# Two mixers: the recurrent branch moved ahead of the last softmax, and two output blocks placed between the attention heads

## The reference

```
z = h @ w_in[l]
xr, yr, q, k, v = jnp.split(z, splits, axis=-1)
lru = rg_lru(causal_conv(xr, conv_w[l], conv_b[l]), gate_a_w[l], ...) * jax.nn.gelu(yr)
att = diff_attention(q, k, v, positions, ...)
x = x + g1 * (jnp.concatenate([lru, att], axis=-1) @ w_out[l])

# rg_lru: r, i sigmoid gates of the convolved x
log_a = -RG_C * r * jax.nn.softplus(-lam)
a = jnp.exp(log_a)
mult = jnp.sqrt(-jnp.expm1(2.0 * log_a))
_, h = lax.associative_scan(_lin_rec, (a, mult * (i * x)), axis=1)

# attention, per head: two softmaxes over masked scores
p = jax.nn.softmax(jnp.where(mask, s, neg), axis=-1)
pd = p[:, :, 0] - lam * p[:, :, 1]
o = rmsnorm(pd @ v, subln_g) * (1.0 - lambda_init)
```

## Time and profile before

| | us |
|---|---|
| median of 3 runs | 2181.72 |
| lowest and highest run | 2180.49, 2182.75 |
| the profiled execution | 2178.4 |
| its span, first instruction to last | 2176.5 |
| TensorE busy in the span | 2032.2 (93%) |
| VectorE busy | 1736.3 (80%) |
| ScalarE busy | 1250.9 (57%) |
| GpSimd busy | 50.0 (2%) |

### The profile page before, as it was taken

One profiled execution on the slowest core, in us unless ns is written; L12 is line 12 of the kernel. 1 busy time (PEld: TensorE's weight loads), 2 busy tenths in 40 slices (PEclk: granted clock), 3 DMA queues, 4 the chain that ended last, 5 costly groups with the idle time before them and its releaser, 6 DMA issues. The chain is left out here.

```text
span 2176.5 us, 31581 instructions
## 1 busy us (share of the span) xinstructions
PE 2032.2 (93%) x12420; PEld 1775.3 (82%) x12421; DVE 1736.3 (80%) x1989; ACT 1250.9 (57%) x1258; POOL 50.0 (2%) x87
## 2 busy tenths in 40 slices
PE   6999998978799989899999879999999999999996
PEld 6889996967699979699988768888888888788885
DVE  6758886786588877678787658898989898889886
ACT  5654444632354455643445647777777777777774
POOL 0000001000000000000000000000000000000000
PEclk9999999997699999999999979999999999999998
DMA  6347861201377634287864229998989898999894
GB/s 247 135 185 283 304 225 64 95 21 40 136 278 264 251 122 173 97 298 292 306 236 141 97 86 352 337 367 337 365 336 366 331 374 331 352 341 374 340 367 171
DMA packets 79069, 534.08 MB, mean 245 GB/s; under 512 B 11648, under 2 KB 13056, under 8 KB 15216
## 3 DMA queue, kind: packets, MB, share of 16 engines
q1 hardware_dynamic: 71440, 481.04, 58.9%
q0 software_dynamic: 7376, 51.25, 6.4%
q10 hardware_dynamic: 144, 0.26, 0.0%
HBM read 531.47 MB, written 1.05 MB: 245 GB/s over the span
## 5 line engine op out<-in xcount | busy, mean ns | idle before, releaser
L2586 DVE TENSOR_TENSOR weights_lo<-ring,weights_hi 128x2048 fp32r<-128x2048 f32 x288 | 656.6, 2291 | 94.7 <-ACT weights_hi L2580 93.0
L2580 ACT CAST weights_hi<-ring 128x2048 fp32r<-128x2048 f32 x288 | 550.8, 1916 | 153.4 <-PE bank L2730 71.6
L658 PE MATMUL bank<-acts_hi,weights_hi 128*128 128x256 f32 x1600 | 460.3, 288 | 17.2 <-DVE acts_lo L395 11.7
L373 DVE TENSOR_TENSOR weights_lo<-ring,weights_hi 128x2048 fp32r<-128x2048 f32 x162 | 370.4, 2290 | 119.0 <-ACT weights_hi L365 117.4
L658 PE MATMUL bank<-acts_lo,weights_hi 128*128 128x256 f32 x1600 | 454.2, 284 | 0.0
L658 PE MATMUL bank<-acts_hi,weights_lo 128*128 128x256 f32 x1600 | 454.1, 284 | 0.0
L365 ACT CAST weights_hi<-ring 128x2048 fp32r<-128x2048 f32 x162 | 308.8, 1909 | 251.0 <-PE bank L658 223.2
L658 PEld LDWEIGHTS bank<-acts_hi,weights_hi 128*128 128x128 f32 x1600 | 305.5, 191 | 24.4 <-issue 18.3
L2730 PE MATMUL bank<-weights_hi,xg_hi 128*128 128x512 f32 x768 | 307.5, 400 | 5.4 <-DVE xg_lo L2850 3.9
L658 PEld LDWEIGHTS bank<-acts_lo,weights_hi 128*128 128x128 f32 x1600 | 305.4, 191 | 2.6 <-issue 1.4
L658 PEld LDWEIGHTS bank<-acts_hi,weights_lo 128*128 128x128 f32 x1600 | 305.2, 191 | 0.0
(11 more groups left out here) (441 smaller groups left out, 2666.4 us busy)
## 6 DMA issues: line engine op xcount, KB each, us to landing
ring<-in_experts SPq DMA_DIRECT2D x288, 1024.0 KB, 5.1
ring<-in_dense SPq DMA_DIRECT2D x162, 1024.0 KB, 4.9
ada<-in_ada POOLq DMA_DIRECT2D x48, 1024.0 KB, 5.1
silu_c<-in_c SPq DMA_DIRECT2D x3, 512.0 KB, 6.3
resid<-in_x SPq DMA_DIRECT2D x1, 1024.0 KB, 6.6
out<-resid SPq DMA_DIRECT2D x2, 512.0 KB, 2.6
cst<-in_consts SPq DMA_DIRECT2D x1, 649.5 KB, 9.1
kh<-in_rwkv_g SPq DMA_DIRECT2D x1, 512.0 KB, 7.2
```

What stands on the lines that cost most here:

```text
L373: nc.vector.tensor_tensor(split[1][:, n % SPLITS, :], ring[:, n % RING, :], split[0][:, n % SPLITS, :].bitcast(F32), ALU.subtract).then_in ...
L658: ins = nc.tensor.matmul(bank[:, f * T:(f + 1) * T], split[w][:, m % SPLITS, k * 256 + f * P:k * 256 + (f + 1) * P], acts[x][:, k, :], sta ...
L2580: nc.scalar.copy(split[0][:, (moe_first + j) % SPLITS, :], ring[:, slot, :]).then_inc(hi_ready, 1)
L2586: nc.vector.tensor_tensor(split[1][:, at, :], ring[:, (moe_first + j) % RING, :], split[0][:, at, :].bitcast(F32), ALU.subtract).then_inc( ...
```

## The change

The whole diff lies in `mixer` and so takes place twice in an execution. It does five things.

1. The steps of the recurrent branch move forward on ScalarE and VectorE. The three passes over `rg` come before the read of Y1 instead of behind it, the square root before the exponentials of head 2, Gelu right behind them. On VectorE the scans come before the mixing of head 2 and the product before that of head 3.
2. The product of scan and Gelu stays in `xc` instead of going to `AT`, so it no longer waits for head 3 to be mixed. ScalarE casts its two parts before and behind the exponentials of head 3; the first cast waits until input block V1 is used up, since it overwrites `acts_hi`.
3. TensorE runs output block one before the turn of head 3 and output block two behind the outputs of heads 2 and 3. Both stood behind all four read-outs.
4. Since output blocks fill banks 4 to 7, turns and outputs move to others: heads 2 and 3 are turned in bank 3 instead of 5, and the outputs of the four heads go to banks 0, 2, 1 and 0 instead of 6, 7, 6 and 7. The turn of head 2 waits for the masks of head 3 to be read from bank 3.
5. Output 0 no longer waits for the last gate read; output block one does.

```diff
@@ -2192,6 +2192,8 @@
                 osq = rc[:].rearrange("p t (h n) -> p t h n", h=4)
                 ov = sb(f"ov{l}", [P, 8], stage=stage)
                 zz = rs
+                turned_to = (pb[5], pb[5], pb[3], pb[3])
+                out_to = (pb[0], pb[2], pb[1], pb[0])
                 ahead(then + 2)
                 norm = norm()
                 with engine_programs() as block:
@@ -2260,22 +2262,24 @@
                                 pe.wait_ge(lru_gate_read, 4 * l + 3)
                             if h:
                                 pe.wait_ge(d_copied, 4 * l + h)
+                            if h == 2:
+                                pe.wait_ge(d_masked, 8 * l + 8)
                             for t in range(TT):
                                 for kt in range(2):
-                                    ins = nc.tensor.transpose(pb[5][:, kt * T + t * P:kt * T + (t + 1) * P],
+                                    ins = nc.tensor.transpose(turned_to[h][:, kt * T + t * P:kt * T + (t + 1) * P],
                                                               Pd[:, h % 2, t * T + kt * P:t * T + (kt + 1) * P], ident)
                             ins.then_inc(d_turned, 1)
 
                         def out(h):
                             pe.wait_ge(win_read, 10 * l + (V0 if h < 2 else V1) + 1)
-                            if h == 0:
-                                pe.wait_ge(lru_gate_read, 4 * l + 4)
                             pe.wait_ge(d_copied, 4 * l + h + 1)
-                            if h >= 2:
-                                pe.wait_ge(d_read, 4 * l + h - 1)
+                            if h == 2:
+                                pe.wait_ge(win_read, 10 * l + V1 + 1)
+                            if h == 3:
+                                pe.wait_ge(d_read, 4 * l + 1)
                             for t in range(TT):
                                 for kt in range(2):
-                                    ins = nc.tensor.matmul(pb[6 + h % 2][:, t * P:(t + 1) * P],
+                                    ins = nc.tensor.matmul(out_to[h][:, t * P:(t + 1) * P],
                                                            PT[:, h % 2, kt * T + t * P:kt * T + (t + 1) * P],
                                                            V[:, kt, h * P:(h + 1) * P], start=(kt == 0), stop=(kt == 1))
                             ins.then_inc(d_out, 1)
@@ -2304,13 +2308,14 @@
                         turn(2)
                         out(0)
                         out(1)
+                        pe.wait_ge(lru_gate_read, 4 * l + 4)
+                        pe.wait_ge(at_lo, 4 * own + 1)
+                        project(pe, n1, 0, 4, acts)
                         turn(3)
                         out(2)
                         out(3)
-                        pe.wait_ge(d_read, 4 * l + 4)
-                        for c in range(2):
-                            pe.wait_ge(at_lo, 4 * own + c + 1)
-                            project(pe, n1 + c, c, 4, acts)
+                        pe.wait_ge(at_lo, 4 * own + 2)
+                        project(pe, n1 + 1, 1, 4, acts)
                         pe.wait_ge(o_norm, l + 1)
                         for h in range(4):
                             for t in range(TT):
@@ -2353,11 +2358,11 @@
                             act.wait_ge(d_turned, 4 * l + h + 1)
                             if h >= 2:
                                 act.wait_ge(d_out, 4 * l + h - 1)
-                            nc.scalar.copy(PT[:, h % 2, :], pb[5][:]).then_inc(d_copied, 1)
+                            nc.scalar.copy(PT[:, h % 2, :], turned_to[h][:]).then_inc(d_copied, 1)
 
                         def read_out(h):
                             act.wait_ge(d_out, 4 * l + h + 1)
-                            nc.scalar.copy(O[:, :, h, :], pb[6 + h % 2][:, 0:2 * P].rearrange("p (t n) -> p t n", t=2)).then_inc(d_read, 1)
+                            nc.scalar.copy(O[:, :, h, :], out_to[h][:, 0:2 * P].rearrange("p (t n) -> p t n", t=2)).then_inc(d_read, 1)
 
                         round_to(act, n0 + 3)
                         for i in (Q0, K0, X0, X1):
@@ -2375,28 +2380,30 @@
                                 ins = nc.scalar.activation((rg, ig)[q // 2][:, ft, :], pb[(6, 7, 5, 6)[q]][:, f * T:(f + 1) * T],
                                                            ACT.Sigmoid, bias=v(("gate_a_b_2", "gate_x_b_2")[q // 2], 4 * l + ft))
                             ins.then_inc(lru_gate_read, 1)
-                        read(Y1)
-                        copy_turned(1)
                         act.wait_ge(lru_log, l + 1)
                         nc.scalar.activation(e2, rg[:], ACT.Exp, scale=2.0)
                         nc.scalar.activation(th, rg[:], ACT.Tanh, scale=-1.0).then_inc(act_step.sem, 1)
                         act_step.n += 1
                         act_step.wait(act)
                         nc.scalar.activation(rg[:], rg[:], ACT.Exp).then_inc(lru_exp, 1)
-                        exps(2)
-                        read(V0)
+                        read(Y1)
+                        copy_turned(1)
                         act.wait_ge(lru_mult, l + 1)
                         nc.scalar.activation(th, th, ACT.Sqrt).then_inc(lru_exp, 1)
+                        exps(2)
+                        act.wait_ge(win_read, 10 * l + Y1 + 1)
+                        nc.scalar.activation(yr[:], yr[:], ACT.Gelu_apprx_tanh).then_inc(lru_exp, 1)
+                        read(V0)
+                        act.wait_ge(used, n0 + V1 + 1)
+                        at_round(act, own, 0, xc)
                         exps(3)
                         read(V1)
                         copy_turned(2)
-                        nc.scalar.activation(yr[:], yr[:], ACT.Gelu_apprx_tanh).then_inc(lru_exp, 1)
+                        at_round(act, own, 1, xc)
                         read_out(0)
                         read_out(1)
                         copy_turned(3)
                         read_out(2)
-                        for c in range(2):
-                            at_round(act, own, c)
                         read_out(3)
                         act.wait_ge(d_read, 4 * l + 4)
                         nc.scalar.activation(osq, O, ACT.Square).then_inc(o_sq, 1)
@@ -2506,28 +2513,27 @@
                         ins.then_inc(lru_log, 1)
                         dve.wait_ge(lru_conv, l + 1)
                         L(nc.vector.tensor_tensor(ig[:], ig[:], xc[:], ALU.mult))
+                        dve.wait_ge(lru_exp, 3 * l + 1)
+                        nc.vector.scalar_tensor_tensor(th, e2, 1.0, th, ALU.add, ALU.mult).then_inc(lru_mult, 1)
                         first_half(2)
                         rest_to(dve, n0 + 11)
-                        dve.wait_ge(lru_exp, 3 * l + 1)
-                        nc.vector.scalar_tensor_tensor(th, e2, 1.0, th, ALU.add, ALU.mult).then_inc(lru_mult, 1)
-                        second_half(2)
-                        first_half(3)
-                        rest_to(dve, n0 + 12)
                         dve.wait_ge(lru_exp, 3 * l + 2)
                         L(nc.vector.tensor_tensor(ig[:], ig[:], th, ALU.mult))
                         for ft in range(4):
                             ins = nc.vector.tensor_tensor_scan(xc[:, ft, :], rg[:, ft, :], ig[:, ft, :], 0.0, ALU.mult, ALU.add)
                         dve_step.mark(ins)
-                        second_half(3)
+                        second_half(2)
+                        first_half(3)
                         dve.wait_ge(lru_exp, 3 * l + 3)
-                        dve.wait_ge(d_mixed, 4 * l + 4)
                         dve_step.wait(dve)
                         for c in range(2):
                             w = slice(2 * c, 2 * c + 2)
-                            nc.vector.tensor_tensor(AT[:, w, :], xc[:, w, :], yr[:, w, :], ALU.mult).then_inc(at_ready[c], 1)
+                            nc.vector.tensor_tensor(xc[:, w, :], xc[:, w, :], yr[:, w, :], ALU.mult).then_inc(at_ready[c], 1)
+                        at_rest(dve, own, 0, xc)
+                        rest_to(dve, n0 + 12)
+                        second_half(3)
+                        at_rest(dve, own, 1, xc)
                         rest_to(dve, n1 + 3)
-                        for c in range(2):
-                            at_rest(dve, own, c)
                         dve.wait_ge(o_sq, l + 1)
                         nc.vector.reduce_sum(ov[:], osq.rearrange("p t h n -> p (t h) n"), AX).then_inc(o_var, 1)
                         dve.wait_ge(o_root, l + 1)
```

## The result

The changed kernel takes 2166.38 us, median of 4 (2164.65 to 2172.86), beside 2182.23 us for the kernel before in the same comparison. The ratio is 0.9921, with a 95% interval of 0.9903 to 0.9939: 15.9 us less by the medians, 17.2 by the ratio. Forecast were 2165.2 us and 16.5 us.

What follows compares the result with a forecast made beforehand. Bound: the chain ScalarE exponential, VectorE mixing, TensorE turn, with two output blocks queued behind it. Gains of 8.04 and 8.50 us make 16.5; 2181.7 - 16.5 = 2165.2 us, range 2162 to 2168.5, chance 0.81.

Steps and rivals of the forecast that it cites:

- The sum: Turn of head 2 to normed-output transposes: TensorE's queued work without waits, 16.04 us for 24.08 and 24.54; 16.5 us gained.
- The ladders: Other engines' times per mixer: block one's operand 0.8 us early, head 3 two us early, norm one us early.
- What follows starts from TensorE's last result: From the normed-output transposes on: order as before, so later work starts earlier by the gain.
- I keep all of it: Behind the mixers: router and expert stream start earlier by the whole gain, so all 16.5 us are kept.
- Rival two: Behind mixer two: granted clock falls elsewhere, 3 us either way, 2162 to 2168.5 us; bad side beyond forecast, chance 0.03.
- Rival one: ScalarE becomes the bound, TensorE waits at block one or output 3; costs 1 to 4 us per mixer; chance 0.12.
- Rival three: Block one: late acts_lo also holds up head 3's turn; 7.5 us late means slower, about 2187 us; chance 0.02.
- Rival four: Rest of the program absorbs the gain and the time doesn't move, 2180 to 2184 us; chance 0.02.
- my signs of being wrong: TensorE waiting at block one or output 3, clock below 1.00 in block one, or later stages over 2 us longer.

Runs made afterwards that it cites:

- both repeats: The changed kernel run again unaltered, twice, against the kernel before: 2168.58 us (ratio 0.9941) and 2168.42 us (ratio 0.9927).
- the six others with the weave in both mixers: Changed kernel plus: ScalarE delayed; five or two idle matmuls; gate group in bank 4; norm in halves; or the last two together (2159.65 us; others only traced).
- the run without the weave: Changed kernel with TensorE's old order, output block one behind the turn of head 3 and all head outputs: 2183.22 us, ratio 0.9999 to the kernel before.
- the two with one mixer: Kernel before with the change in one mixer only: mixer one 2175.16 us (ratio 0.9973), mixer two 2174.58 us (ratio 0.9961).

## Why the prediction was right

**The sum.** The steps were right and came to a little too much: 24.08 and 24.54 us became 15.67 and not 16.04. Turn of head 2 to turn of head 3 took 7.81 us where the steps made 8.02, and from there to the transposes 7.86, where they made 8.02. The step that was mis-sized is the outputs of two heads: 1.95 us is the time to the end of the last of them, but the next matmul starts 1.71 us behind their start (886.11 to 887.82). The block itself takes 5.66 (887.82 to 893.48), where I had 5.63. Gain in the stretch 17.3 us, forecast 16.5. A part of it is clock, which the sum took in without saying so: 2.85 of mixer one's 8.41 us.

**The ladders.** All three hold: the operand of block one 0.6 us early (forecast 0.8), head 3 mixed before block one ends (turn at 893.48, Pd made at 891.93), the norm done at 900.54, 0.80 us before the transposes (forecast 1.0). ScalarE's slack was tested by putting 3 us in, and the 1.4 us that it cost are the ladder's total, though not its split.

**What was missed.** "What follows starts from TensorE's last result" and "I keep all of it" was the step that failed, by 1.56 us a fall. Rival two was the right mechanism at the wrong place: I looked for the clock behind mixer two, where TensorE has holes of its own, and it fell at block three, in a hole of 2.22 us that had never cost anything before. Seven falls in eight mixers make 2.7 us of an execution, and 17.28 - 2.7 = 14.6. The medians of both repeats give 14.6 and the first comparison 15.9; by the ratios the three are 12.9, 15.9 and 17.2, so the agreement to a tenth is chance, and that 2165.2 came within 1.2 us of 2166.38 is in part luck. The gain was taken 0.7 us too small, the falls of 2.7 us were left out, and the first comparison came out 1.3 us better than the repeats. The run-to-run spread was also larger than the 1 us either way of the forecast: the kernel before took 2176.33 to 2189.29 us in 26 executions.

**Rival one** didn't come: no ScalarE step held TensorE up, the added table load included. The load took 1.28 us and the pass behind it began 0.02 later (874.35 + 1.28, and 875.65 in ScalarE's timeline), as the trace of before had it. By the Trainium skill, "ScalarE: Activation LUTs", "What ACT_TABLE_LOAD costs", a drain of about 1380 ns comes on top of each load; the runs show none. **Rival three**, slower by a late operand, needed one 7.5 us late; it was 0.6 us early. **Rival four**, that the rest absorbs it, looked partly true in the first profile, where the experts took 8.5 us more; that also was one of my signs of being wrong, a later stage longer by more than 2 us. Over thirteen profiles the expert stretch took 882.4 to 893.0 us, with 11.5 to 91 us of waits for DMA. The changed kernel itself had 893.0, 887.8 and 891.0, the six others with the weave in both mixers 884.1, 882.4, 892.4, 884.1, 887.3 and 886.2, the run without the weave 889.6, and the two with one mixer 886.1 and 885.8. So the stretch varies by 10 us among kernels whose code there is the same, and with the weave it can be as short as before. The kernel before has one profile only (884.5), shorter than six of the nine with the weave, and the medians' intervals are some 4 us wide to each side. So a loss of a few us in the experts that comes with the change is neither shown nor excluded.

## What to carry to other kernels

Where an engine idles for a result that others make, look in its own queue for work behind the wait that needs nothing from it, and then ask which memory and which banks tie that work to the wait; here it was a scratch memory shared with the scores and two banks. Work out a ladder of the other engines' times before moving it: with durations from the trace it was right to some 0.2 us over some twenty steps. For pipelined matmuls take a row's distance to the next start, not its length. And compare stages, not spans, when one stage is fed by a stream that varies by more than the gain.

## What the runs showed of the hardware

In the changed kernel TensorE works for 15.7 us without a gap, stands for 2.2 us and goes on with dense matmuls. There the granted clock went down to half, 1.2 GHz, for some 3 us in seven of eight mixers, at a cost of 1.55 us. With the hole filled, cut to 0.5 us or gone it did so in none of eight, but with the same hole behind other work in none of ten either.

Each load of a ScalarE table took 1.28 us, and the next pass began 0.02 us behind its end (874.35 + 1.28, then 875.65).

A matmul of two plain float32 operands of 512 columns takes 0.78 us here and shows as two records, against 0.23 for one whose operands are split parts (five in 3.9 us, and the rows of block three).

The stretch that streams experts at some 340 to 360 GB/s took 882.4 to 893.0 us in thirteen profiles in which its code is the same.
